# Retention in head pairs, V-products written turned, and the group norm moved into the gate

## The chip, the cores and the metric

One Trainium2 chip, of which the kernel uses one core. The metric is device time in microseconds (us) of one execution. In the profile PE is TensorE, PEld its weight load, DVE is VectorE, ACT is ScalarE, POOL is GpSimd and SP the queue that issues the weight transfers.

## The reference, cut to what matters

Two blocks of a transformer run over 256 positions of width 1024. The last quarter holds the layer around the change: a latent attention (MLA) of 8 heads and a two-directional retention of 8 heads, both fed by one input projection, joined before one output projection.

```python
proj = rms_norm(h, mix_norm) @ w_in           # c_q, c_kv, k_pe, r_q, r_k, r_v, r_g
# MLA, for each of 8 heads (q, k of 96, v of 64)
p = softmax((q_nope @ k_nope.T + q_pe @ k_pe.T) * MLA_SCALE)      # 256 x 256
a = p @ v
# retention, for each of 8 heads of 64: decayed scores, forward and backward in one mask
o = (q @ k.T * 64 ** -0.5 * decay) @ v_r
o = (o - mean(o)) * rsqrt(var(o) + EPS)       # over the 64 values of a head
r = silu(r_g) * o
h = h + concat([a, r]) @ w_o
h = h + 0.5 * swiglu_2(rms_norm(h, ffn2_norm), ...)               # FFN4, the last phase
```

All is float32. A product with a weight is made as three passes over a high and a low part.

## The kernel before, in words

Rows are in two tiles t = 0, 1 of 128. Each phase is a list of steps, `walk_latent` for the layer above; every engine walks the same list and issues, in that order, what it has to do in a step. So the list fixes the order of work on each engine, and a wait in a step holds everything behind it on that engine.

Weights come in chunks of 128 x 1024. SP fills 4 raw buffers, and issues the transfer for chunk c + 4 when chunk c has been split. A refill step ("R" for one chunk) makes on ACT `w_high` (L1035) and then on DVE `w_low` (L1301); the ring of split chunks has 12 places, and `freed` lists chunks that TensorE has used with row tile 1, whose places wait for a refill. Counted from the first chunk of the latent layer, its input projections use chunks 0 to 22, `w_o` chunks 23 to 30, FFN4's first gate-and-up block 31 to 34, the second 35 to 38, and the first down block 39 and 40.

Steps of the layer: X(i, t, c) is one chunk of an input projection (6 matmuls of 512 columns); MS(v), v = 0 to 7, the MLA scores of two heads of one row tile, into the PSUM tile `pG[v % 2]`; on DVE MS takes the row maxima (L1539, L1542); ME(v) the exponentials on ACT (L1238) into `mp`; MPT(v) turns `mp` on TensorE (L1641) and copies it (L1548, DVE); MPV(v) multiplies by V (L1913); MN(t) divides four products by the softmax sums at once; MAT(t) turns them and splits high from low. The loop over v issues:

```python
            for v in range(8):
                if v < 7: step("ME", v + 1)
                step("MPT", v)
                # one or two X chunks
                if v < 6: step("MS", v + 2)
                if v >= 1: step("MPV", v - 1)
```

with a refill at the start and after MS. After it follow RT (turn q and k of the retention), `decay` (3 exponentials on ACT and one product on POOL for each head), RS (scores of a head, L1939), RM (times the decay, DVE, L1569), RPV (times V, L1952), the group norm on DVE (GNmean, GNvar, GNout), RAT (turn the result, split), and between them Oc(t, kt), the output projection, one chunk each. RROPE is the rotation of q and k on POOL.

The program emits each float32 product as two TensorE instructions, so a count of x8 below stands for four products; a transposition, and each pass of a product with a weight, is one.

Of the kernel before, what the change touches and what calls it, by code (L numbers as in the profile page):

```python
# [27 lines left out]
F32 = mybir.dt.float32  # L28
# [7 lines left out]
P = 128  # L36
# [68 lines left out]
CONSTS = C_REL + 4 * P  # L105
# [302 lines left out]
def walk_latent(step, freed, open_end):  # L408
# [33 lines left out]
    step("MT", 0)  # L442
    projects(2, 1)
    step("U", 1)
    step("exp_table",)
# [11 lines left out]
    beside = [(3, 1, c) for c in range(1, 4)] + [(4, 0, c) for c in range(4)] + [(4, 1, c) for c in range(4)]  # L457
    project(*beside.pop(0))
    refill(step, freed, 1)
    for v in range(8):  # L460
        refill(step, freed, 1)
        if v < 7:
            step("ME", v + 1)
        step("MPT", v)
        for _ in range(min(1 + v % 2, len(beside))):
            project(*beside.pop(0))
        if v < 6:
            step("MS", v + 2)
        refill(step, freed, 1)
        if v == 6:  # L470
            step("gate", 0)
        if v == 7:
            step("RT", 0)
            step("MAT", 0)
# [6 lines left out]
    step("MN", 1)  # L481
    step("gate", 1)
    step("decay", 0)
    step("decay", 1)
    output(0, 0)
    step("MAT", 1)
    refill(step, freed)
    for hd in range(2, 8):
        step("decay", hd)
    step("silu",)  # L490
    step("RS", 0)
    step("RS", 1)
    for hd in range(8):
        step("RM", hd)
        if hd == 0:
            output(0, 1)
        step("RPV", hd)
        if hd < 6:
            step("RS", hd + 2)
        if hd == 4:  # L500
            step("GNmean", 0)
    step("GNvar", 0)
    step("GNmean", 1)
    step("GNvar", 1)
    step("GNout", 0)
    step("GNout", 1)
    for kt in range(2, 4):
        output(0, kt)
    for kt in range(3):
        output(1, kt)  # L510
    step("RAT", 0)
    output(1, 3)
    step("RAT", 1)
    refill(step, freed)
# [60 lines left out]
def build(nc, x_in, stream, consts_in, table_in, pos_in, posts_in, out):  # L575
    with ExitStack() as ctx:
# [75 lines left out]
        ttmp = [place(f"ttmp{i}", [P, 8, RHALF], F32, lat_at + i * 1024 if i < 3 else None) for i in range(4)]  # L652
# [3 lines left out]
        mo = [place(f"mo{t}", [P, 512], F32, mq_at + t * MLA_HEADS * QK * 4) for t in range(2)]  # L656
        mv = [place(f"mv{t}", [P, 512], F32) for t in range(2)]
        rqk_both = place("rqk", [P, 2, 1024], F32)
# [4 lines left out]
        sd = [place(f"sd{i}", [P, 2, SEQ], F32, p_at + i * 2 * SEQ * 4) for i in range(2)]  # L663
# [4 lines left out]
        dm_at = [lat_at, lat_at + 1536] + [mkT_at + 1536 * i for i in range(5)] + [mpT_at + 2048]  # L668
# [8 lines left out]
        rel = consts[:, C_REL:C_REL + 4 * P]  # L677
# [56 lines left out]
        x_out, lat_ss, lr_ready = (rows2(n) for n in ("x_out", "lat_ss", "lr_ready"))  # L734
        latT_psum, latf_ready, lath_ready, latT_ready = (rows2(n) for n in ("latT_psum", "latf_ready", "lath_ready", "latT_ready"))
        u_out, mqk_ready, mT_psum = (rows2(n) for n in ("u_out", "mqk_ready", "mT_psum"))
# [3 lines left out]
        mo_ready = rows2("mo_ready")  # L740
        rrope_done = rows2("rrope_done")
        rT_psum, rqT_ready, rkT_ready = rows2("rT_psum"), rows2("rqT_ready"), rows2("rkT_ready")
        dm_exp, dm_ready, rot_part = sem("dm_exp"), sem("dm_ready"), sem("rot_part")
        rs_psum, sd_ready, rpv_done = sem("rs_psum"), sem("sd_ready"), sem("rpv_done")
        rgate, silu_ready = rows2("rgate"), sem("silu_ready")
        gn_var, gn_r, ro_ready = sem("gn_var"), sem("gn_r"), sem("ro_ready")
# [101 lines left out]
        def _(pool):  # L848
# [114 lines left out]
            def LAT(t, ph):  # L963

                pool.wait_ge(lat_ss[t], 2)
                link(pool.tensor_scalar(lms[t][:, 0:1], lss[t][:, 0:1], 1.0 / Q_RANK, EPS, ALU.mult, ALU.add))
                link(pool.tensor_scalar(lms[t][:, 1:2], lss[t][:, 1:2], 1.0 / KV_RANK, EPS, ALU.mult, ALU.add))
                pool.tensor_tensor(lrr[t], lms[t], half_neg[:, 0:2], ALU.pow).then_inc(lr_ready[t], 1)

            def U(t, ph):  # L970
                if t == 1:

                    pool.wait_ge(latT_psum[1], 1)
                    pool.wait_ge(mqk_ready[1], 2)
# [22 lines left out]
            def GNvar(part, ph):  # L997

                g = gn[part]
                pool.wait_ge(gn_var, part + 1)  # L1000
                link(pool.tensor_scalar(g[:, 2, :], g[:, 1, :], 1.0 / HD, EPS, ALU.mult, ALU.add))
                pool.tensor_tensor(g[:, 3, :], g[:, 2, :], half_neg, ALU.pow).then_inc(gn_r, 1)
# [9 lines left out]
            steps = {f.__name__: f for f in (start, parts, finish, tail, rope, S, LAT, U, RROPE, decay, GNvar)}  # L1012
# [9 lines left out]
        def _(sc):  # L1022
# [178 lines left out]
            def LAT(t, ph):  # L1201
                sc.wait_ge(x_out[t], 1)
                sc.activation(junk[t][:, 0:Q_RANK], lat[t][:, 0:Q_RANK], ACT.Square, accum_out=lss[t][:, 0:1]).then_inc(lat_ss[t], 1)
                sc.activation(junk[t][:, Q_RANK:Q_RANK + KV_RANK], lat[t][:, Q_RANK:Q_RANK + KV_RANK], ACT.Square,
                              accum_out=lss[t][:, 1:2]).then_inc(lat_ss[t], 1)
                sc.wait_ge(latf_ready[t], 1)
                if t == 1:
                    sc.wait_ge(u_done0, 1)
                sc.activation(latTh[:], latf[:], ACT.Copy).then_inc(lath_ready[t], 1)

            def U(t, ph):
                if t == 1:
                    sc.wait_ge(w_freed, C_U + 3)
                    sc.wait_ge(mT_psum[0], 2)
                else:
                    sc.wait_ge(u_done0, 1)
                sc.wait_ge(lr_ready[t], 1)
# [7 lines left out]
            def MT(t, ph):  # L1225
                sc.wait_ge(mT_psum[t], 1)
# [4 lines left out]
            def ME(v, ph):  # L1231
                t, j = v // 4, v % 4
                sc.wait_ge(mmax_ready, v + 1)
# [6 lines left out]

            def RT(t, ph):
# [854 lines left out]
```

## Time and profile before

| | us |
|---|---|
| median of 3 runs | 1067.25 (1066.87 to 1067.92) |
| profiled execution, time | 1068.99 |
| profiled execution, span of the trace | 1067.1 |
| PE busy | 1056.3 (99%) |
| PEld busy | 873.2 (82%) |
| DVE busy | 656.3 (62%) |
| ACT busy | 559.4 (52%) |
| POOL busy | 104.8 (10%) |

The span runs from the first to the last instruction; the time of the execution also holds what lies around it, 1.9 us here. Busy time is the union of an engine's instructions. Matmuls are pipelined, so two in a row overlap and the distance of their starts is what one costs; the chain view shows these shares alone.

### The profile page before, as it was taken

How to read it: one execution, taken by the hardware profiler on the slowest of the kernel's cores; microseconds unless marked ns; L12 is line 12 of the kernel's file. 1: busy time of each engine (PE TensorE's matmuls, PEld its weight loads, DVE VectorE, ACT ScalarE, POOL GpSimd, SP SyncE). 2: the span in 40 equal slices, each digit the busy share in tenths (PEclk: the TensorE clock that was granted, in tenths of full speed). 3: DMA queues.
4: the chain of work that ended last, by engine and by line, in shares of the span. 5: the costliest groups of instructions: out<-in, count | busy, mean ns of one | idle time of the engine just before them, and what ended most of it. 6: DMA issues, size and time to landing. Idle time of an engine off the chain costs nothing.

```text
span 1067.1 us, 14824 instructions
## 1 busy us (share of the span) xinstructions
PE 1056.3 (99%) x5047; PEld 873.2 (82%) x5047; DVE 656.3 (62%) x932; ACT 559.4 (52%) x905; POOL 104.8 (10%) x194
## 2 busy tenths in 40 slices
PE   9999999999999999999999999999999999999997
PEld 6999888888877788888888888888888888888886
DVE  5867754546687775554667555466668674655544
ACT  5755644535677654454555445455576544444542
POOL 0035000000022040000000000000026110000001
PEclk9999999999999999999999999999999999999999
DMA  8563656555552354645555464555545133646441
GB/s 339 181 241 128 211 167 214 174 180 201 192 194 102 119 195 160 216 170 184 196 198 188 164 218 172 182 196 198 178 158 178 61 128 109 213 161 215 169 147 40
DMA packets 51884, 187.81 MB, mean 176 GB/s; under 512 B 5808, under 2 KB 5952, under 8 KB 51840
## 3 DMA queue, kind: packets, MB, share of 16 engines
q1 hardware_dynamic: 50688, 183.79, 49.5%
q0 software_dynamic: 864, 3.07, 1.0%
q8 instruction: 27, 0.44, 0.2%
q10 hardware_dynamic: 288, 0.37, 0.1%
q14 instruction: 17, 0.14, 0.0%
HBM read 186.15 MB, written 1.05 MB: 175 GB/s over the span
## 4 chain that ended last, share of the span: by engine, by line
PE 94%; DVE 3%; ACT 1%; issue 0%; DMA 0%; POOL 0%; POOLq 0%; DVEq 0%; SPq 0%; ACTq 0%
PE pG L1636 17%; PE pG L1638 17%; PE pG L1637 17%; PE pD L1636 11%; PE pD L1638 11%; PE pD L1637 11%; PE pT L1641 3%; DVE w_low L1301 1%; PE pG L1641 1%; PE pG L1658 1%; PE pT L1952 1%; PE pG L1939 1%; PE pD L1913 1%; PE pT L1779 1%; PE pD L1641 1%; PE pG L1894 1%
## 5 line engine op out<-in xcount | busy, mean ns | idle before, releaser
L1301 DVE TENSOR_TENSOR w_low<-raw,w_high 128x1024 fp32r<-128x1024 f32 x340 | 412.6, 1232 | 119.6 <-ACT w_high L1035 107.3
L1035 ACT ACTIVATE w_high<-raw 128x1024 fp32r<-128x1024 f32 x340 | 351.5, 1055 | 78.4 <-PE pG L1638 66.5
L1636 PE MATMUL pG<-w_high,xTh 128*128 128x512 f32 (+1 forms) x816 | 320.3, 393 | 0.1
L1638 PE MATMUL pG<-w_high,xTl 128*128 128x512 f32 (+1 forms) x816 | 312.7, 383 | 0.0
L1637 PE MATMUL pG<-w_low,xTh 128*128 128x512 f32 (+1 forms) x816 | 312.2, 383 | 0.0
L1638 PEld LDWEIGHTS pG<-w_high,xTl 128*128 128x128 f32 x816 | 153.2, 188 | 28.2
L1637 PEld LDWEIGHTS pG<-w_low,xTh 128*128 128x128 f32 x816 | 153.7, 188 | 25.6
L1636 PEld LDWEIGHTS pG<-w_high,xTh 128*128 128x128 f32 x816 | 153.3, 188 | 25.6 <-DVE xTl L1334 0.4
L1636 PE MATMUL pD<-w_high,aTh 128*128 128x512 f32 x384 | 150.9, 393 | 0.0
L1638 PE MATMUL pD<-w_high,aTl 128*128 128x512 f32 x384 | 150.0, 390 | 0.0
L1637 PE MATMUL pD<-w_low,aTh 128*128 128x512 f32 x384 | 149.5, 389 | 0.0
L1120 ACT ACTIVATE gate<-pG,stat 128x256 f32<-128x256 f32 x104 | 49.2, 474 | 169.2 <-PE pG L1638 167.0
L1140 ACT ACTIVATE aTh<-pT 128x256 fp32r<-128x256 f32 x88 | 33.7, 383 | 150.8 <-PE pT L1641 150.8
L1440 DVE TENSOR_TENSOR aTl<-pT,aTh 128x256 fp32r<-128x256 f32 x88 | 37.3, 424 | 119.0 <-ACT aTh L1140 119.0
L1421 DVE SCALAR_TENSOR_TENSOR act<-pG,stat,gate 128x256 f32<-128x256 f32 x88 | 42.3, 481 | 95.7 <-ACT gate L1120 95.6
L1638 PEld LDWEIGHTS pD<-w_high,aTl 128*128 128x128 f32 x384 | 72.1, 188 | 15.1
L1636 PEld LDWEIGHTS pD<-w_high,aTh 128*128 128x128 f32 x384 | 72.1, 188 | 14.1
L1637 PEld LDWEIGHTS pD<-w_low,aTh 128*128 128x128 f32 x384 | 72.2, 188 | 14.1
L1636 PE MATMUL pD<-w_high,xTh 128*128 128x512 f32 (+1 forms) x160 | 64.6, 404 | 0.0
L1638 PE MATMUL pD<-w_high,xTl 128*128 128x512 f32 (+1 forms) x160 | 62.0, 388 | 0.0
L1637 PE MATMUL pD<-w_low,xTh 128*128 128x512 f32 (+1 forms) x160 | 61.8, 386 | 0.0
L1641 PE MATMUL pT<-consts,act 128*128 128x128 f32 x192 | 37.8, 271 | 0.2 <-DVE act L1421 0.2
(266 smaller groups left out, 834.1 us busy)
## 6 DMA issues: line engine op xcount, KB each, us to landing
raw<-in_stream SPq DMA_DIRECT2D x340, 512.0 KB, 4.3
post<-in_posts POOLq DMA_DIRECT2D x5, 512.0 KB, 5.1
early<-in_stream SPq DMA_DIRECT2D x4, 512.0 KB, 12.0
first_w<-in_stream SPq DMA_DIRECT2D x3, 512.0 KB, 5.4
h<-in_x SPq DMA_DIRECT2D x2, 512.0 KB, 5.0
out<-hg SPq DMA_DIRECT2D x3, 256.0 KB, 2.3
consts<-in_consts POOLq DMA_DIRECT2D x1, 416.0 KB, 4.6
out<-hg ACTq DMA_DIRECT2D x1, 256.0 KB, 2.7
```

Source lines behind the costliest of these rows:

```text
L1035: sc.activation(w_high[:, slot(static):slot(static) + CHUNK], raw_of(static), ACT.Copy).then_inc(w_high_done, 1)
L1120: sc.activation(gate[t][:], pG[t][:, 0:256], ACT.Copy if ph.mixer else ACT.Silu, scale=rr[t]).then_inc(gate_ready[t], 1)
L1140: sc.activation(aTh[t][:].rearrange("p k r -> p (k r)"), pT[t][:, 0:256], ACT.Copy).then_inc(ah_ready[t], 1)
L1301: ve.tensor_tensor(w_low[:, slot(static):slot(static) + CHUNK], raw_of(static), w_high[:, slot(static):slot(static) + CHUNK].bitcast(F32), ...
L1421: ve.scalar_tensor_tensor(act[t][:], pG[t][:, 256:512], rr[t], gate[t][:], ALU.mult, ALU.mult).then_inc(act_ready[t], 1)
L1440: ve.tensor_tensor(aTl[t][:].rearrange("p k r -> p (k r)"), pT[t][:, 0:256], aTh[t][:].rearrange("p k r -> p (k r)").bitcast(F32), ALU.sub ...
L1636: pe.matmul(dst, ah, hi, start=start, stop=False)
L1637: pe.matmul(dst, ah, lo, start=False, stop=False)
L1638: return pe.matmul(dst, al, hi, start=False, stop=stop)
L1641: return pe.transpose(dst, src, ident)
L1658: mm = pe.matmul(pG[t][:, 0:MIX.cols], hg[t][:, kt * P:(kt + 1) * P], first_w[:, kt * MIX.cols:(kt + 1) * MIX.cols], start=kt == 0, stop=k ...
L1779: mm = pe.matmul(pT[p][:, P * keys * x:P * keys * (x + 1)], qT[t][part, 4 * a + first + x, :], kT[part, a, 0:P * keys], start=True, stop=True)
```

## The change

Four things are done together in the latent layer.

1. RS and RPV take two heads in one step. The scores alternate between the row halves of the array (heads 2i and 2i+1 lie on partitions 0 to 63 and 64 to 127), the products with V between the column halves, with V as the stationary operand and 256 moving columns, so that the result is written turned. MPV is written turned in the same way, with 128 moving columns; MAT needs no turning any more, and the transpositions of the MLA result go.
2. The softmax sums then lie on the wrong axis, so MN(v) divides `mp` before it is turned, for each v: a reciprocal of 128x2 and a product of 128x512 on DVE, and MPT(v) on TensorE waits for it. The copy of the turned `mp` moves from DVE to ACT.
3. V of the retention is centred over the head before it is used (VC: a reduction and a scaling on DVE, a subtraction on POOL). The variance is made from squares (ACT) by TensorE products with a column of 1/64 (VAR); the inverse root goes into the gate, the gate is turned (GT), and RY multiplies it by the turned product.
4. The list of steps is written anew: one X chunk in a turn of the loop instead of one or two, refills only after the odd turns, four X chunks between the retention steps, `decay` for four heads inside the loop, RROPE between the projections, and refills limited to given numbers later on.

```diff
     step("LAT", 0)
+    step("RROPE", 0, 0)
...
     step("U", 0)
+    step("RROPE", 0, 1)
...
     projects(3, 0)
+    step("VC", 0)
     step("MT", 1)
-    for t in range(2):
-        for part in range(2):
-            step("RROPE", t, part)
     project(3, 1, 0)
...
-    beside = [(3, 1, c) for c in range(1, 4)] + [(4, 0, c) for c in range(4)] + [(4, 1, c) for c in range(4)]
+    beside = [(3, 1, c) for c in range(1, 4)] + [(4, 0, c) for c in range(4)]
     project(*beside.pop(0))
     refill(step, freed, 1)
     for v in range(8):
-        refill(step, freed, 1)
         if v < 7:
             step("ME", v + 1)
+        step("MN", v)
         step("MPT", v)
-        for _ in range(min(1 + v % 2, len(beside))):
+        for _ in range(min(1, len(beside))):
             project(*beside.pop(0))
         if v < 6:
             step("MS", v + 2)
...
         if v >= 1:
             step("MPV", v - 1)
-        if v == 4:
-            step("MN", 0)
+        if v == 3:
+            step("VC", 1)
+        if 2 <= v < 6:
+            step("decay", v - 2)
+        if v == 6:
+            step("MAT", 0)
+        refill(step, freed, v % 2)
+    step("RT", 0)
+    step("gate", 0)
     step("MPV", 7)
+    project(4, 1, 0)
     step("RT", 1)
+    project(4, 1, 1)
+    step("decay", 4)
+    step("decay", 5)
+    step("RS", 0)
+    step("RM", 0)
+    project(4, 1, 2)
+    step("decay", 6)
+    step("RPV", 0)
+    step("RS", 1)
+    step("RM", 1)
+    step("decay", 7)
+    project(4, 1, 3)
+    step("RPV", 1)
+    step("RS", 2)
     step("gate", 1)
+    step("SQ", 0)
+    step("RM", 2)
+    step("MAT", 1)
     output(0, 0)
...
+    step("RPV", 2)
+    step("RS", 3)
+    step("RM", 3)
     step("silu",)
...
+    output(0, 1)
+    step("VAR", 0)
     step("GNvar", 0)
...
+    step("RPV", 3)
+    step("SQ", 1)
+    step("GNout", 0)
+    refill(step, freed, 1)
+    output(0, 2)
+    step("VAR", 1)
     step("GNvar", 1)
...
+    output(0, 3)
     step("GNout", 1)
...
+    refill(step, freed, 1)
     for kt in range(3):
         output(1, kt)
-    step("RAT", 0)
+    step("GT", 0)
+    step("RY", 0)
     output(1, 3)
-    step("RAT", 1)
-    refill(step, freed)
+    step("GT", 1)
+    step("RY", 1)
+    step("RL", 0)
+    step("RL", 1)
+    refill(step, freed, 2)
     for kt in range(4, 8):
         output(0, kt)
...
+            def MN(v, ph):
+                t, j = v // 4, v % 4
+                ve.wait_ge(mp_ready, 2 * (v + 1))
+                chain(ve.reciprocal(lrec[t][:, 2 * j:2 * j + 2], lsum[t][:, 2 * j:2 * j + 2]))
                 joined()
...
+                ve.tensor_tensor(mp[v % 2][:], mp[v % 2][:], lrec[t][:, 2 * j:2 * j + 2].unsqueeze(2).broadcast_to([P, 2, SEQ]),
+                                 ALU.mult).then_inc(mn_ready, 1)
...
             def MPT(v, ph):
-                pe.wait_ge(mp_ready, 2 * (v + 1))
+                pe.wait_ge(mn_ready, v + 1)
...
+                for kt in range(2):
+                    for x in range(2):
+                        hd = 2 * j + x
+                        mm = pe.matmul(pD[t][HD * x:HD * (x + 1), 512 + P * j:512 + P * (j + 1)], mv[kt][:, HD * hd:HD * (hd + 1)],
+                                       mpT[v % 2][:, (2 * x + kt) * P:(2 * x + kt + 1) * P], start=kt == 0, stop=kt == 1)
...
+            def RS(i, ph):
...
                 for jt in range(2):
...
+                    for x in range(2):
+                        part = slice(HD * x, HD * (x + 1))
+                        mm = pe.matmul(pG[x][:, SEQ * jt:SEQ * (jt + 1)], rkT[part, i, P * jt:P * (jt + 1)], rqT[part, i, :],
+                                       start=True, stop=True)
...
+            def VAR(part, ph):
...
+                for i in range(2):
+                    for t in range(2):
+                        first = 8 * part + 4 * t + 2 * i
+                        mm = pe.matmul(pD[1][:, first:first + 2], sq[part][:, SEQ * i + P * t:SEQ * i + P * (t + 1)], half_mean,
+                                       start=True, stop=True)
```

`refill(step, freed, n)` refills at most n chunks of `freed`, and without n all of them; the first such full refill of FFN4 stands in its first step, `walk_block_step(ph, 0)`, behind T(0, 0), the turning of the first activation of row tile 0.

## Rows read from the trace of the kernel before

**Rows 1.** The page: busy time of each engine, and the chain's shares by engine

```profile
PE 1056.3 (99%) x5047; PEld 873.2 (82%) x5047; DVE 656.3 (62%) x932; ACT 559.4 (52%) x905; POOL 104.8 (10%) x194
PE 94%; DVE 3%; ACT 1%; issue 0%; DMA 0%; POOL 0%; POOLq 0%; DVEq 0%; SPq 0%; ACTq 0%
```

**Rows 2.** Busy time by stretch; columns: us, PE, PEld, DVE, ACT, POOL (instructions), PEclk, DMA share, GB/s

```profile
798.00:834.00 36.00, 35.86 (x218) 31.34 (x218) 31.18 (x42) 22.13 (x50) 20.18 (x19) 1.00 0.49 175
...
1050.00:1067.00 17.00, 10.43 (x53) 8.67 (x51) 7.62 (x16) 4.76 (x12) 3.06 (x3) 0.94 0.17 63
```

**Rows 3.** The chain that ended last, three stretches; columns: start us, us, what

```profile
355.46 1.06 PE pT L1779 x8
356.52 1.01 PE pG L1804 x8
...
811.47 0.87 PE pG L1894 x4
812.33 0.84 PE pD L1913 x8
813.17 0.44 PE pT L1641 x4
...
841.43 1.06 PE pG L1939 x4
842.49 1.03 PE pT L1952 x8
```

**Rows 4.** Timeline of PE in the MLA loop; start us, us, engine, line, operation

```profile
801.71 0.66 PE L1641 MATMUL pT<-consts,mp 128*128 128x128 f32 x4
...
809.48 0.61 PE L1641 MATMUL pT<-consts,mp 128*128 128x128 f32 x4
...
811.31 1.03 PE L1894 MATMUL pG<-mkT,mqT 96*128 96x256 f32 x4
...
819.75 1.03 PE L1894 MATMUL pG<-mkT,mqT 96*128 96x256 f32 x4
```

**Rows 5.** Timeline of DVE in the same loop

```profile
802.64 2.89 DVE L1301 TENSOR_TENSOR w_low<-raw,w_high 128x1024 fp32r<-128x1024 f32 x2 [0.66 <-ACT w_high L1035]
...
820.82 0.69 DVE L1539 TENSOR_REDUCE mx<-pG 128x2 f32<-128x512 f32 x1 [1.25 <-PE pG L1894]
...
821.62 1.22 DVE L1301 TENSOR_TENSOR w_low<-raw,w_high 128x1024 fp32r<-128x1024 f32 x1
822.75 0.20 DVE L1552 RECIPROCAL lrec<-lsum 128x8 f32<-128x8 f32 x1
822.99 0.69 DVE L1555 TENSOR_TENSOR mo<-pD,lrec 128x512 f32<-128x512 f32 x1
```

**Rows 6.** Timelines, hand-overs: DVE to PE, then PE to ACT

```profile
834.44 0.69 DVE L1555 TENSOR_TENSOR mo<-pD,lrec 128x512 f32<-128x512 f32 x1
...
835.18 0.66 PE L1641 MATMUL pD<-consts,mo 128*128 128x128 f32 x4 [0.22 <-DVE mo L1555]
...
859.63 0.66 PE L1641 MATMUL pG<-consts,rqk 128*128 128x128 f32 x4
...
860.33 0.60 ACT L1278 ACTIVATE xTh<-pG 128x512 fp32r<-128x512 f32 x1 [15.27 <-PE pG L1641]
```

**Rows 7.** Timelines: start of Oc(0, 4), then the start of FFN4

```profile
861.87 0.48 PE L1636 MATMUL pD<-w_high,xTh 128*128 128x512 f32 x1
...
880.64 0.48 PE L1636 MATMUL pG<-w_high,xTh 128*128 128x512 f32 x1
...
888.92 0.38 PE L1641 MATMUL pT<-consts,act 128*128 128x128 f32 x2
...
883.04 1.05 ACT L1035 ACTIVATE w_high<-raw 128x1024 fp32r<-128x1024 f32 x1
...
884.12 1.22 DVE L1301 TENSOR_TENSOR w_low<-raw,w_high 128x1024 fp32r<-128x1024 f32 x1 [0.53 <-ACT w_high L1035]
```

**Rows 8.** The page: weight transfers, KB each, median us to landing

```profile
raw<-in_stream SPq DMA_DIRECT2D x340, 512.0 KB, 4.3
```

More of the change, by code:

```diff
@@ L442, in walk_latent @@
     step("MT", 0)
+    step("RROPE", 1, 0)
     projects(2, 1)
     step("U", 1)
+    step("RROPE", 1, 1)
     step("exp_table",)
@@ L651, in build @@
         lat = [place(f"lat{t}", [P, LATENT], F32) for t in range(2)]
-        ttmp = [place(f"ttmp{i}", [P, 8, RHALF], F32, lat_at + i * 1024 if i < 3 else None) for i in range(4)]
+        at[0] = lat_at + 4 * P * 8
         mq_at = at[0]
@@ L655, in build @@
         mk = place("mk", [P, MLA_HEADS, QK], F32)
-        mo = [place(f"mo{t}", [P, 512], F32, mq_at + t * MLA_HEADS * QK * 4) for t in range(2)]
+        mv_at = at[0]
         mv = [place(f"mv{t}", [P, 512], F32) for t in range(2)]
+        sq = [place(f"sq{i}", [P, 512], F32, mv_at + 2048 * i) for i in range(2)]
+        roS = place("roS", [P, 4, SEQ], F32, lat_at)
         rqk_both = place("rqk", [P, 2, 1024], F32)
@@ L666, in build @@
         mpT = [place(f"mpT{i}", [P, 4 * P], F32) for i in range(2)]
[L668 removed]
+        sd = [place(f"sd{i}", [P, 2, 2, SEQ], F32, p_at + i * 4096) for i in range(2)]
+        yo = [place(f"yo{t}", [P, 512], F32, p_at + 2048 * t) for t in range(2)]
+        ttmp = [place(f"ttmp{i}", [P, 8, RHALF], F32, (p_at + 2048, p_at + 3072, mpT_at + 2048, mpT_at + 3072)[i]) for i in range(4)]
+        dm_at = [mq_at + 1536 * i for i in range(4)] + [mkT_at + 1536 * i for i in range(4)]
         dm = [place(f"dm{i}", [P, 3 * P], F32, dm_at[i]) for i in range(8)]
@@ L1010, in finish @@
                 pool.tensor_tensor(rr[1], ms[1], half_neg[:, 0:1], ALU.pow).then_inc(end_r, 1)
-            steps = {f.__name__: f for f in (start, parts, finish, tail, rope, S, LAT, U, RROPE, decay, GNvar)}
+            steps = {f.__name__: f for f in (start, parts, finish, tail, rope, S, LAT, VC, RROPE, decay, GNvar)}
             in_loop = ("G", "D", "T", "Y", "R")
@@ L1938, in RS @@
+            def RS(i, ph):
+                if i == 0:
+                    pe.wait_ge(rqT_ready, 2)
+                    pe.wait_ge(rkT_ready, 2)
+                else:
+                    pe.wait_ge(sd_ready, 4 * i)
                 for jt in range(2):
-                    mm = pe.matmul(pG[hd % 2][:, SEQ * jt:SEQ * (jt + 1)], rkT[part, hd // 2, P * jt:P * (jt + 1)],
-                                   rqT[part, hd // 2, :], start=True, stop=True)
+                    for x in range(2):
+                        part = slice(HD * x, HD * (x + 1))
+                        mm = pe.matmul(pG[x][:, SEQ * jt:SEQ * (jt + 1)], rkT[part, i, P * jt:P * (jt + 1)], rqT[part, i, :],
+                                       start=True, stop=True)
@@ L1956, in MAT @@
-            def MAT(t, ph):
-                pe.wait_ge(mo_ready[t], 1)
-                for k in range(4):
-                    mm = turned(pD[t][:, 512 + P * k:512 + P * (k + 1)], mo[t][:, P * k:P * (k + 1)])
-                mm.then_inc(catT_psum[t], 1)
-            def RAT(t, ph):
-                pe.wait_ge(ro_ready, 2)
-                for k in range(4):
-                    mm = turned(pG[t][:, P * k:P * (k + 1)], rqk[t][:, P * k:P * (k + 1)])
+                    pe.wait_ge(vc_ready, 2)
@@ new lines, in RPV @@
+                for jt in range(2):
+                    for x in range(2):
+                        hd = 2 * i + x
+                        mm = pe.matmul(pT[i // 2][HD * x:HD * (x + 1), SEQ * (i % 2):SEQ * (i % 2 + 1)], rv[jt][:, HD * hd:HD * (hd + 1)],
+                                       sd[i % 2][:, x, jt, :], start=jt == 0, stop=jt == 1)
+                mm.then_inc(rpv_done, 1)
+            def VAR(part, ph):
+                pe.wait_ge(sq_ready, part + 1)
+                if part == 0:
+                    pe.wait_ge(rgate, 2)
+                else:
+                    pe.wait_ge(gn_var, 1)
+                for i in range(2):
[3 more added lines that the diff above has]
+                                       start=True, stop=True)
+                mm.then_inc(var_psum, 1)
@@ L1977, in _ @@
             steps = dict(start=start, turn=turn, first=first, G=G, D=Dn, T=T, proj=proj, QKT=QKT, S=S, PT=PT, PV=PV, O=O, X=X, LAT=LAT_,
-                         U=U, MT=MT, MS=MS, MPT=MPT, MPV=MPV, RT=RT, RS=RS, RPV=RPV, MAT=MAT, RAT=RAT, Oc=Oc)
+                         U=U, MT=MT, MS=MS, MPT=MPT, MPV=MPV, RT=RT, RS=RS, RPV=RPV, VAR=VAR, GT=GT, Oc=Oc)
             walk(pe, lambda name, *a, ph=None: steps[name](*a, ph) if name in steps else None)
@@ L2061, in shape_constants @@
     dist = j - i
-    c[:, C_REL:C_REL + 4 * P] = np.concatenate(
+    c[:, C_REL:C_HALF] = np.concatenate(
         [np.maximum(dist, 0), dist + P, np.maximum(-dist, 0), P - dist], axis=1)
+    for x in range(2):
+        c[HD * x:HD * (x + 1), C_HALF + x] = 1.0 / HD
     return c
```

258 lines of the change are left out of this document (105 added, 153 removed).

## The prediction

> **What bounds the kernel now.** I read the page first. TensorE is busy in 99% of the span and holds 94% of the chain that ended last; DVE is busy in 62%, ACT in 52% [rows 1]. Then the stretches around the change: in the MLA loop (798 to 834 us) PE is busy in 35.86 of 36 us at the full granted clock, while DVE is close behind with 31.18 and POOL works 20.18 [rows 2]. So the kernel runs as long as TensorE's instructions take, as long as nothing they wait for is late. The change must be read twice: what TensorE's work becomes, and whether what feeds it still comes in time. For the first I take the chain view, which gives what each group costs alone; for the second the timelines of PE and DVE, with each engine's steps in the order of the new list.
>
> **TensorE's work.** Scores of one head cost 1.06 us (x4), the product with V of one head 1.03 (x8) [rows 3]. The attention of the first block already alternates halves of the array: there twice as many instructions of the same width cost 1.06 (row halves) and 1.01 (column halves, 256 moving columns) [rows 3]. So RS goes from 8 x 1.06 to 4 x 1.06, a gain of 4.2 us, and RPV from 8 x 1.03 to 4 x 1.01, 4.2. MPV, now 0.84, has no like: 128 moving columns in column halves. Below it stands half of 0.84, 0.42, above it 0.84; I take 0.6: four instructions of 256 columns cost 0.87, so eight of 128 would too; half of it is 0.44, and the attention's pair lies 0.14 above its own half (1.01 against 0.87) [rows 3]. That gives 8 x 0.24 = 1.9. MAT's eight transpositions go, 2 x 0.44 = 0.9 [rows 3]. VAR adds 2 x 8 instructions whose stationary operand is 128 x 128 and which hardly move a column; the nearest row is MPV's 0.84 for 8, so +1.7 (at the least 0.4, if nearly all of that were columns). GT replaces RAT one for one. Sum: 4.2 + 4.2 + 1.9 + 0.9 - 1.7 = 9.5 us less for TensorE.
>
> Between whole array and halves a changeover shows: four score instructions of the retention (half the rows) cost 1.06 beside MLA's 0.87, and RPV 1.03 beside MPV's 0.84, 0.19 each [rows 3]. The Trainium skill, TensorEngine Tiling (Array Packing), Key Properties, says that changing the tiling mode drains TensorE. That speaks against a change that puts a column-half product into each turn of a loop of whole-array work; my 0.6 has 0.14 of it, and by that rule, with a drain at both edges, it would be 8 x 0.19 = 1.5 us more, six of the eight in the shadow of the wait below.
>
> **The new wait in the MLA loop.** Before, MPT(v) needed only the exponentials. Now it needs MN(v), and DVE works in the order of the list: MN(v), MS(v+2), on odd turns a refill, MN(v+1). The row maxima of MS(v+2) cannot begin before TensorE has made these scores, and MN(v+1), whose exponentials are long ready, is queued behind them; behind MPT(v+1) on TensorE is queued everything else. One turn, from MPT(v) to MPT(v+1):
> - MPT(v), one X chunk, start of MS(v+2): 811.31 - 809.48 = 1.83 [rows 4];
> - start of MS to the maxima on DVE: 820.82 - 819.75 = 1.07; maxima and scaling to the next DVE instruction: 0.80 [rows 4, 5];
> - reciprocal to product 0.24; product 0.69, the same size as mo's; hand-over to PE 0.05 [rows 5, 6].
>
> Sum 4.68 us. TensorE's work in it is 1.83 + 0.87 + 0.6 = 3.3, so it stands about 1.4 us in each turn. A refill between adds 1.13 (821.62 to 822.75) in the turns that follow v = 1, 3, 5; VC(1) at v = 3 adds 0.80, by the like pair of instructions. MPT(0) to MPT(6): 6 x 4.68 + 3 x 1.13 + 0.80 = 32.3 us. ACT (exponentials, copy, decay, w_high) has about 3.5 of work a turn, so it is not what ends.
>
> The start is late too: refill 24 stands before MN(0) on DVE. It began at 802.64 and holds 1.13, so MPT(0) starts at 802.64 + 1.13 + 0.24 + 0.69 + 0.05 = 804.75, where it started at 801.71 [rows 4, 5]. MN(6) is done at 804.7 + 32.3 = 837.0.
>
> **From MN(6) to Oc(0, 4).** At v = 6 DVE has MAT(0)'s low part ahead of MN(7), and that waits for ACT, whose copies wait for MPT(6): hand-over 0.05, PE to ACT 0.70 (859.63 to 860.33), two ACT copies 0.50 and 0.60, 0.05, low part 0.60, MN(7) 0.24 + 0.69 + 0.05 = 3.5 us until MPT(7) [rows 5, 6]. From there the work of TensorE rules, since four X chunks and the Oc chunks lie between the retention steps: transpositions of MPT(7), RT and GT 7 x 0.44 = 3.1; MPV 2 x 0.6 = 1.2; 12 chunks of 1.40 (1.83 less 0.44 for the turning) = 16.8; RS 4.2; RPV 4.0; VAR 1.7; 31.0 in all. Waits beside it: RT(1), whose banks are copied behind refill 28, 0.3; the handing over between RS, RM and RPV, 0.6; and RL(0), the low part that Oc(0, 4) needs, which is queued on DVE behind RY(1) and so behind GT(1): 0.70 + 0.60 + 0.69 + 0.05 less the turning, 1.6. Together 3.5 + 31.0 + 2.5 = 37.0, so Oc(0, 4) starts at 874.0 instead of 861.87 [rows 7]. That is +12.1 us, with the 9.5 us of saved work already in it: the waits take some 21.
>
> **The refills put off.** Counting `freed` along both lists: before, the layer splits up to chunk 41 ahead of FFN4's first block; after, at the same place, only up to 35, and the full refill behind T(0, 0) then does seven, 36 to 42, where it did one. The second gate-and-up block needs 36 at once. In before's time (880.64 the start of that block, 888.92 T(0, 1)) [rows 7]: chunk 35 lasts until 882.1; w_high of 36 begins at 883.04 and w_low ends at 884.12 + 1.22 = 885.3, a stall of 3.2. Chunks 37 to 39 lie in the raw buffers and come each 1.13. The transfer for 40 goes out when 36 is split, lands 4.3 later [rows 8], and after 1.06 and 1.22 is ready at 891.9; PE has come to it at 890.8. Chunk 42 follows at 894.2, and only behind it in DVE's queue stands the activation that T(0, 1) turns: 894.2 + 0.48 + 0.05 = 894.7 for 888.92. That is +5.8; if the transfers were there already it would be 3.8, with a landing 1 us slower 6.9. FFN4 is bound by TensorE and gives nothing back.
>
> **Moved at no cost.** RROPE on POOL now lies beside the projections; LAT(1) is queued behind two of its four parts on POOL, which fit between the projections, and it takes POOL off the loop, where two w_low took 2.89 instead of 2.3 [rows 5] (all of it lies in the 20.18 us of POOL [rows 2]). If LAT(1) were late it would cost one part, some 5 us. VC on POOL and four `decay` on ACT lie in the shadow of the waits. SP issues the same transfers in the same order, the constants grow by two columns.
>
> **Sum.** +12.1 + 5.8 = +17.9. Against the profiled execution that is 1068.99 + 17.9 = 1086.9 (its span 1067.1 + 17.9 = 1085.0); it ran 1.7 above the median, so against the median 1067.25 + 17.9 = 1085.2. I say 1085. Its own range is 1080 to 1090, from the bounds above (MPV and VAR 1, the transfers 2 down and 1 up, contention of VC(1) with DVE 0.6, waits in the retention 2).
>
> **Rivals.**
> - *Arithmetic alone.* TensorE has its maxima and MN early enough, and only its work counts: 1067.25 - 9.5 = 1057.8, faster. It decides if a turn from MPT to MPT stays at 3.3 to 3.4 us, so if DVE's part after MS took 0.6 instead of 2.85. The busy shares speak for it (DVE 62%), the order of DVE's queue against it. Chance 7%.
> - *The loop is late, the refills are hidden.* The seven refills find cover in FFN4 (DVE is busy a good half of the time): 1067.25 + 12.1 = 1079.4. It would need T(0, 1) not to stand behind chunk 42. 12%.
> - *The clock falls.* All through the loop the granted clock is 1.00, which is 2.4 GHz; at the end of the kernel, once TensorE has finished, it is 0.94 in the mean [rows 2]. If it went to 1.2 GHz for the six turns, PE's share of a turn, 1.83 + 0.87, would double: 6 x 2.7 = 16.2 on top, 1101. The stalls are of 1.4 to 3.5 us with work between them. The Trainium skill, TensorE: Matmul & The Clock Gate, the section on HAM oscillation, has repeated waits throttle the array; no stretch of before with such waits shows it. 6%.
> - *More late than I see*: a wait on ACT, LAT(1), or in the retention, some 5 to 8 us on top: 1092. 10%.
> - The forecast, 65%.
>
> **Numbers.** The measurement tells a difference from none at about 0.2% (2.1 us). Faster 8%: the arithmetic case and a little for gains I have not counted. Same 2%: it would need both delays to be a third of what I count. Slower 90%. The range reaches from 1077 (the refills hidden, with a margin) to 1093 (one more wait), and leaves out the clock and the arithmetic case.
>
> **What would show it.** In the trace after: starts of `pT<-consts,mp` 4.7 us apart, 5.8 after odd turns, each with PE idle until DVE `mp`; MPV about 0.6; RS and RPV x8 at about 1.05; 12 us more to the start of Oc(0, 4); seven w_low in a row behind the first activation of FFN4, with PE idle for 3 us in `pG`. Wrong it would be if the MPT starts lay 3.4 apart, or if the DVE product on `mp` came before the maxima of the next scores.

## The result, and the profile after

The changed kernel took 1097.22 us (median of 4, 1095.22 to 1098.18) beside 1067.59 for the kernel before (median of 4, 1066.87 to 1068.48): a ratio of 1.0275, with an interval of 1.0257 to 1.0293. The forecast was 1085, with a range to 1093; the direction was right, the size was not: +29.6 us instead of +17.9. The profiled execution took 1097.25 us, with a span of 1095.3.

The page, busy time and the chain's shares by engine, to be read against [rows 1]:

```profile
PE 1059.1 (97%) x5023; PEld 867.6 (79%) x5023; DVE 658.3 (60%) x932; ACT 567.8 (52%) x917; POOL 105.1 (10%) x194
PE 89%; DVE 7%; ACT 2%; issue 1%; DMA 1%; POOL 0%; POOLq 0%; ACTq 0%; DVEq 0%; SPq 0%
```

TensorE has 24 instructions less, yet it is busy for longer. DVE had 3% of the chain and now has 7%. What TensorE waited for between 740 and 930 us (columns: engine and line, releaser: us in total, times, longest):

```profile
PE pT L1663 <- DVE mp L1588: 17.5, 8, 3.8
PE pG L1658 <- DVE w_low L1340: 3.1, 1, 3.1
PE pT L1663 <- DVE act L1460: 2.3, 2, 2.1
PE pG L1663 <- DVE mq L1552: 1.7, 1, 1.7
PE pD L1658 <- DVE xTl L1644: 1.4, 1, 1.4
```

That is 26.0 us of waits with DVE as the releaser. All eight MPT wait for MN's product on `mp`. PE's timeline of three turns (against [rows 4]):

```profile
805.50 0.66 PE L1663 MATMUL pT<-consts,mp 128*128 128x128 f32 x4 [2.81 <-DVE mp L1588]
...
810.19 0.66 PE L1663 MATMUL pT<-consts,mp 128*128 128x128 f32 x4 [1.78 <-DVE mp L1588]
810.60 0.48 PE L1658 MATMUL pD<-w_high,xTh 128*128 128x512 f32 x1
810.91 0.59 PE L1659 MATMUL pD<-w_low,xTh 128*128 128x512 f32 x1
811.30 0.63 PE L1660 MATMUL pD<-w_high,xTl 128*128 128x512 f32 x1
811.72 0.63 PE L1658 MATMUL pD<-w_high,xTh 128*128 128x512 f32 x1
...
813.00 1.70 PE L1916 MATMUL pG<-mkT,mqT 96*128 96x256 f32 x4
...
817.62 1.01 PE L1663 MATMUL pT<-consts,mp 128*128 128x128 f32 x4 [2.33 <-DVE mp L1588]
```

The first turn, from MPT(0) to MPT(1), lasts 4.69 us. In the second the matmuls of the X chunk come to start 0.42 apart, where at the full clock it is 0.23, and MS(3) lasts 1.70, where it lasts 1.03 in the kernel before [rows 4]. Busy time by stretch (columns as in [rows 2]; the last but two is the granted clock):

```profile
811.00:813.00 2.00, 2.00 (x6) 1.54 (x5) 0.00 (x0) 0.48 (x1) 0.00 (x0) 0.50 0.00 0
...
822.00:831.00 9.00, 4.20 (x31) 3.03 (x30) 5.68 (x11) 4.56 (x13) 2.39 (x2) 1.00 0.03 5
831.00:834.00 3.00, 2.84 (x10) 2.36 (x11) 0.10 (x1) 1.57 (x4) 0.68 (x2) 0.57 0.44 160
...
846.00:850.00 4.00, 3.38 (x18) 2.72 (x19) 1.22 (x2) 1.68 (x3) 0.00 (x0) 0.50 0.00 0
```

0.50 is the lower level, 1.2 GHz. TensorE falls to it behind some of the waits, and the work of that turn takes nearly twice as long; in other turns it keeps 1.00, which is 2.4 GHz. The DVE timeline shows the order in the queue that makes the wait (against [rows 5]): maxima first, then reciprocal and product.

```profile
808.45 0.69 DVE L1578 TENSOR_REDUCE mx<-pG 128x2 f32<-128x512 f32 x1 [3.00 <-PE pG L1916]
...
809.25 0.16 DVE L1586 RECIPROCAL lrec<-lsum 128x2 f32<-128x2 f32 x1
809.44 0.69 DVE L1588 TENSOR_TENSOR mp<-mp,lrec 128x512 f32<-128x512 f32 x1
```

**A common zero.** Executions differ by up to 2 us before the layer begins. So all starts below count from the layer's first instruction on TensorE, the turning of h: 741.57 us before, 740.71 after. In the timeline after, these are the starts that the table uses:

```profile
740.71 0.60 PE L1663 MATMUL pG<-consts,h 128*128 128x128 f32 x4
...
846.62 1.11 PE L1663 MATMUL pT<-consts,mp 128*128 128x128 f32 x4 [2.11 <-DVE mp L1588]
...
882.81 0.50 PE L1658 MATMUL pD<-w_high,xTh 128*128 128x512 f32 x1 [1.38 <-DVE xTl L1644]
...
917.13 0.44 PE L1663 MATMUL pT<-consts,act 128*128 128x128 f32 x2 [2.08 <-DVE act L1460]
```

Starts in us after that zero, from one profiled execution each; MPT(0) to MPT(7) is the loop, T(0, 1) the place in FFN4 behind which nothing differs any more:

| kernel | MPT(0) | MPT(7) | Oc(0, 4) | T(0, 1) | time, median |
|---|---|---|---|---|---|
| before | 60.1 | 87.5 | 120.3 | 147.4 | 1067.6 |
| after | 64.8 | 105.9 | 142.1 | 176.4 | 1097.2 |
| sums first | 64.8 | 87.9 | 121.7 | 156.0 | 1076.9 |
| gaps filled | 64.8 | 101.3 | 135.1 | 169.2 | 1089.5 |
| refills earlier | 64.8 | 109.3 | 145.8 | 172.9 | 1089.1 |
| rotation small | 62.9 | 105.6 | 141.8 | 175.5 | 1095.4 |
| chunk behind scores | 64.8 | 100.5 | 135.8 | 169.6 | 1091.4 |
| two mended | 64.8 | 87.9 | 121.7 | 148.8 | 1070.7 |
| four mended | 60.8 | 83.9 | 118.2 | 145.3 | 1065.9 |
| halves in turn | 60.8 | 83.9 | 118.3 | 145.4 | 1064.9 |
| same half | 60.8 | 83.9 | 120.1 | 147.2 | 1069.0 |
| refill ahead of decay | 60.8 | 83.1 | 115.8 | 142.9 | 1063.8 |

The difference at T(0, 1), 29.1 us, is the whole of what was measured (29.6). Against the forecast: up to MPT(0) 4.65 instead of 3.0, from there to Oc(0, 4) 17.15 instead of 9.1, from there to T(0, 1) 7.27 instead of 5.8. So 11.2 us are to be explained on top of the 17.9, and the 17.9 themselves are to be tested.

### The profile page after: what moved, and what is told of

It reads as the page before. It is cut to its first block, busy times and chain, and to the rows that moved or that the text cites. A ratio compares the mean times of both kernels' runs of the same rounds, so it can differ in the third digit from the quotient of the medians.

```text
span 1095.3 us, 14788 instructions
## 1 busy us (share of the span) xinstructions
PE 1059.1 (97%) x5023; PEld 867.6 (79%) x5023; DVE 658.3 (60%) x932; ACT 567.8 (52%) x917; POOL 105.1 (10%) x194
## 4 chain that ended last, share of the span: by engine, by line
PE 89%; DVE 7%; ACT 2%; issue 1%; DMA 1%; POOL 0%; POOLq 0%; ACTq 0%; DVEq 0%; SPq 0%
PE pG L1658 16%; PE pG L1660 16%; PE pG L1659 16%; PE pD L1658 11%; PE pD L1660 10%; PE pD L1659 10%; DVE w_low L1340 3%; PE pT L1663 3%; PE pG L1680 1%; PE pG L1663 1%; ACT w_high L1058 1%; PE pG L1916 1%; PE pT L1801 1%; DVE mp L1588 1%; DMA raw<-in_stream 1%
```

## The experiments

Ten kernels were run. Beside them the kernel before had medians of 1067.5 to 1068.0, and the ratios are to those. "After" is the changed kernel.

**1. Sums first.** MN(v + 1) stands ahead of MS(v + 2), so that on DVE the product no longer waits behind the maxima.

```diff
+    step("MN", 0)
     for v in range(8):
...
-        step("MN", v)
         step("MPT", v)
...
             project(*beside.pop(0))
+        if v < 7:
+            step("MN", v + 1)
         if v < 6:
             step("MS", v + 2)
```

> The changed kernel with one step moved: the division MN(v+1) stands in the list ahead of the row maxima of MS(v+2), so on VectorE it no longer waits for scores that TensorE has not made. Theory A (the queue order on VectorE is what makes TensorE stand in the loop): turns of 3.3 to 3.7 us instead of 4.7 to 7.4, MPT(0) to MPT(7) about 25 us instead of 41.1, the granted clock back to 1.00 in the loop, and the time 15 to 18 us below that of the changed kernel, 1079 to 1082. Theory B (VectorE or ScalarE has too much work in a turn, whatever the order): turns stay above 4.5 us and the time within 3 us of 1097. If only the clock were at fault and the stalls harmless, it would gain at most the 6 us that the slow stretches of the loop cost.

Measured: 1076.85 us (1076.09 to 1077.11), ratio 1.0081 (1.0064 to 1.0098), 20.4 less than after. PE's timeline:

```profile
805.52 0.66 PE L1665 MATMUL pT<-consts,mp 128*128 128x128 f32 x4 [2.80 <-DVE mp L1590]
...
808.26 0.60 PE L1665 MATMUL pT<-consts,mp 128*128 128x128 f32 x4
...
811.63 0.66 PE L1665 MATMUL pT<-consts,mp 128*128 128x128 f32 x4
```

Turns of 2.7 to 3.8 us instead of 4.7 to 7.4; between 804 and 846 us PE is busy for 38.48 us at a clock of 1.00, where it was 26.41 at 0.87. The place of one step in the list cost two thirds of the loss. It is more than the waits that vanished: PE waited 17.5 us for `mp` and now waits 4.8, 12.7 less. The other 7.7 us, which also put the time below the 1079 to 1082 that I expected, are a second effect that the waits bring about, and the next run looks for it.

**2. Gaps filled.** The list is that of after; 37 useless products of 128x256, whose results nobody reads, run on TensorE in its waits.

```diff
         if v >= 1:
             step("MPV", v - 1)
+        step("gap", v)
...
+                for _ in range({-1: 6, 0: 3, 1: 5, 2: 3, 3: 8, 4: 3, 5: 5, 6: 4}.get(v, 0)):
+                    pe.matmul(dst, ident, rel[:, 0:256], start=True, stop=True)
```

> The changed kernel with useless products (128x128 by 256 columns, 0.43 us each, results never read) put on TensorE into the places of the loop where it stands: 3, 5, 8 or 6 of them according to the wait, 37 in all. No wait is taken away. Theory A (the clock fell because TensorE stood, and cost time on top of the stalls): the granted clock stays at 1.00 up to the first retention step, the turns return to the 4.7, 5.8 and 6.6 us worked out at the full clock, and the time falls by 6 to 9 us, to 1088 to 1091, although TensorE has 16 us more work. Theory B (the longer turns come from contention or a slower ScalarE, and the clock only shows it): the time stays at 1097 or rises by up to 3 us.

Measured: 1089.53 us (1089.29 to 1089.72), ratio 1.0202 (1.0185 to 1.0219). With work added, it is 7.7 us faster than after. The stretches of the loop, first of after, then of this kernel:

```profile
804.00:846.00 42.00, 26.41 (x136) 19.68 (x136) 16.83 (x35) 18.52 (x50) 4.18 (x5) 0.87 0.15 51
```
```profile
804.00:846.00 42.00, 40.99 (x240) 31.27 (x239) 18.44 (x35) 20.85 (x52) 4.18 (x5) 1.00 0.16 52
```

The clock stays at 1.00, and the turns last 4.69, 5.84, 4.83, 7.19, 4.83 and 5.76 us, 33.1 in all for a forecast of 32.3 (4.68, 5.81, 4.68, 6.61, 4.68, 5.81). So the wait was sized rightly. Of the 0.8 us between, 0.65 is one instruction: in the turn with VC(1) the product on `mp` takes 1.34 us instead of 0.69, beside VC's and decay's work on POOL, here as in after:

```profile
829.76 1.34 DVE L1588 TENSOR_TENSOR mp<-mp,lrec 128x512 f32<-128x512 f32 x1
```

The clock cost 37.8 - 33.1 = 4.6 us in the loop and, from MPT(7) to Oc(0, 4), 36.2 - 33.8 = 2.4: 7.0 together; the medians have 7.7. The Trainium skill, TensorE: Matmul & The Clock Gate, the section on HAM oscillation, tells of a loop whose waits, for a DMA and of some 3 to 5 us, throttle the array anew each time. The trace agrees that such waits do it, but here they are for VectorE, most are shorter (1.2 to 3.8 us), and the clock does not fall behind each of them. In FFN4 it falls too, behind the wait for `w_low` (0.59 in 906 to 909 us of after), but there the chain of after runs over the transfer and the refills, and TensorE waits again at T(0, 1), so the lower clock costs nothing that shows.

**3. Refills earlier.** A refill behind each of four retention steps, and all that are left behind RL(1), so that FFN4 finds its chunks split.

```diff
     step("decay", 7)
+    refill(step, freed, 1)
     project(4, 1, 3)
     step("RPV", 1)
+    refill(step, freed, 1)
...
     step("RL", 1)
-    refill(step, freed, 2)
+    refill(step, freed)
```

> The changed kernel with four refills put between the retention steps and a full refill after RL, so that chunks up to 41 are split before FFN4's first block, as in the kernel before. Theory A (the seven refills behind the first activation of FFN4 cost TensorE two stalls and a stretch of slow clock): from Oc(0, 4) to T(0, 1) of FFN4 27 us instead of 34.3, and the time 6 to 7.5 us lower, 1090 to 1091. Theory B (the delay is made up elsewhere, or the refills now hold up the retention on VectorE): within 2 us of 1097, or up to 3 us above.

Measured: 1089.05 us (1086.5 to 1093.26), ratio 1.0189 (1.0172 to 1.0206), 8.2 less than after. The wait for `w_low` is gone, and that for `act` is 0.2 instead of 2.3; `mp` keeps its 17.3. From Oc(0, 4) to T(0, 1) it takes 27.1 us, as before (27.05), where after took 34.3: the burst of refills cost 7.2 us, and FFN4 covers none of it. The profiled execution was the slowest of the four, and its clock was 0.76 between 804 and 846 us, with the list of the loop unchanged; its first turn, from MPT(0) to MPT(1), took 7.17 us where after took 4.69. The four executions of this one kernel go from 1086.5 us at a mean clock of 0.994 to 1093.26 at 0.986. The clock doesn't fall at the same waits in each execution.

**4. Rotation small.** RROPE on POOL rotates one head of eight and leaves the others as they are; its steps stay in their places.

```diff
+                z, co, si = z[:, 0:1, :], co[:, 0:1, :], si[:, 0:1, :]
```

> The changed kernel with the rotation on GpSimd cut to one head of eight (the other heads of the retention stay unrotated): its 24 instructions shrink from 128x256 to 128x32 elements and no longer lie beside VectorE's work of U(1) and MT(1). Theory A (GpSimd's early rotation slows VectorE there and makes TensorE stand 1.7 us ahead of MT(1)): that stall goes and the time falls by 1.5 to 2.5 us, to about 1095. Theory B (the stall has another cause, the reordered projections): no change beyond 0.5 us.

Measured: 1095.42 us (1094.3 to 1097.41), ratio 1.0253 (1.0236 to 1.0271), 1.8 less than after. The four times overlap with those of after (1095.22 to 1098.18), so the medians alone don't show the gain; the trace does. MPT(0) starts at 62.9 instead of 64.8, 1.9 earlier, and that is the 1.7 us of PE's wait for `mq`; at T(0, 1) 1.0 of it is left in this execution. What made it is in the DVE timeline of after; the groups have 4 and 1 instructions:

```profile
783.77 6.78 DVE L1340 TENSOR_TENSOR w_low<-raw,w_high 128x1024 fp32r<-128x1024 f32 x4 [0.16 <-ACT w_high L1058]
790.47 0.70 DVE L1546 TENSOR_TENSOR mpT<-lat,trig 128x16 f32<-128x16 f32 x1
...
793.59 0.82 DVE L1547 TENSOR_TENSOR mpT<-mq,trig 128x128 f32<-128x128 f32 x1
```

and in that of the kernel with the small rotation:

```profile
784.89 2.36 DVE L1341 TENSOR_TENSOR w_low<-raw,w_high 128x1024 fp32r<-128x1024 f32 x2 [0.16 <-ACT w_high L1059]
...
792.66 0.28 DVE L1548 TENSOR_TENSOR mpT<-mq,trig 128x128 f32<-128x128 f32 x1
```

Beside POOL a `w_low` takes 1.7 us instead of 1.2, and of the six operations of 128x128 behind them two take 0.82 and 0.81, while the other four take 0.28 or 0.29 as in the small rotation. The Trainium skill, GPSIMD Engine Reference, Specifications, has GpSimd's memory interface shared with VectorE, in contention with instructions of two inputs; these have two, and the trace agrees.

**5. Chunk behind scores.** A weaker cure for the wait than the first: the X chunk of a turn goes behind MS(v + 2), so that the maxima can begin 1.4 us earlier.

```diff
         step("MPT", v)
-        for _ in range(min(1, len(beside))):
-            project(*beside.pop(0))
         if v < 6:
             step("MS", v + 2)
+        for _ in range(min(1, len(beside))):
+            project(*beside.pop(0))
```

> The changed kernel with another mend of the loop: the X chunk stands behind MS(v+2) instead of ahead of it, so that TensorE has 1.4 us of work while VectorE makes maxima and division; the order on VectorE stays as changed. Theory A (a turn is the chain MPT, MS, maxima, refill, division, and the chunk lay in it): turns of 3.3 to 3.5 us without a refill, 4.4 with one and about 5.3 with VC(1), MPT(0) to MPT(7) 27 to 29 us instead of 41.1, and the time 12 to 14 us below 1097, but 4 to 7 above the run with the division first. Theory B (the order of the maxima and the division alone matters): turns hardly shorter than 4.7 us.

Measured: 1091.44 us (1089.7 to 1092.9), ratio 1.0227 (1.0212 to 1.0243), only 5.8 less than after. I expected 12 to 14, with 27 to 29 us from MPT(0) to MPT(7); it took 35.7. Only the first turn shrinks as it should, to 3.7. The other two without a refill take 5.0 and 5.1 for an expected 3.3 to 3.5, though TensorE doesn't wait for `mp` in them: the clock is at its lower level for much of each.

```profile
816.00:820.00 4.00, 4.00 (x13) 2.86 (x11) 1.62 (x4) 2.59 (x8) 0.45 (x1) 0.57 0.39 135
828.00:832.00 4.00, 4.00 (x20) 2.92 (x19) 1.62 (x4) 2.38 (x8) 0.46 (x1) 0.73 0.01 3
```

The turns with a refill take 7.3, 6.0 and 5.3, for 4.4, 5.3 (with VC(1)) and 4.4. ACT and DVE of the second turn:

```profile
811.91 0.69 ACT L1222 ACTIVATE rv<-pD,stat 128x512 f32<-128x512 f32 x1 [1.83 <-PE pD L1660]
812.50 1.04 ACT L1058 ACTIVATE w_high<-raw 128x1024 fp32r<-128x1024 f32 x1
```
```profile
813.58 1.23 DVE L1340 TENSOR_TENSOR w_low<-raw,w_high 128x1024 fp32r<-128x1024 f32 x1 [2.15 <-ACT w_high L1058]
...
814.91 0.69 DVE L1588 TENSOR_TENSOR mp<-mp,lrec 128x512 f32<-128x512 f32 x1
```

The chunk that was put later ends an input projection, whose result ACT copies (`rv`); behind that copy ACT has `w_high`, behind `w_high` DVE has `w_low`, and behind it stands the product. In the sixth turn no such copy stands there, and the chain runs over ACT all the same: copy of the turned `mp`, three exponentials of `decay`, `w_high`, then `w_low` and the product. My expectation moved the chunk on TensorE and forgot what stands ahead of `w_high` on ACT: the same error as in the change itself, one engine further. And it had no term for the clock.

**6. Two and four mended.** The first is experiments 1 and 3 together. The second adds: refill 24 behind MS(2) instead of ahead of MN(0), RL(0) ahead of GT(1), and the last part of RROPE behind the rotation of `mq` and `mk`. So the second, called "four mended", differs from after in five places.

```diff
     project(*beside.pop(0))
-    refill(step, freed, 1)
     step("MN", 0)
...
             step("MS", v + 2)
+        if v == 0:
+            refill(step, freed, 1)
...
+    step("RL", 0)
     step("GT", 1)
     step("RY", 1)
-    step("RL", 0)
     step("RL", 1)
...
+                if t == 1 and part == 1:
+                    pool.wait_ge(mqk_ready[1], 2)
```

> The changed kernel with the division ahead of the row maxima (20.4 us by itself) and the refills between the retention steps (8.2 us by itself) together. Theory A (two separate delays, which add): the second still takes its two stalls and its slow stretch away, 6 to 8 us, so 1069 to 1071, within 0.4% of the kernel before. Theory B (the delays share a cause, such as the clock, so that the second is worth less once the first is gone): 1073 to 1077.

> As the run with both mended, and three small moves: refill 24 behind the first division instead of ahead of it, RL(0) ahead of GT(1) and RY(1), and the last quarter of GpSimd's rotation held until VectorE has done its own rotation for the MLA keys and queries. The stalls of TensorE that are left there are 2.8, 1.4 and 1.7 us. Theory A (each is a wait on the chain, and TensorE's saved 9.5 us then come through): 4 to 5 us below the run with both mended, 1064 to 1066, so just below the kernel before. Theory B (the held rotation runs into the exponentials or slows VectorE's refills at the start of the loop): no more than 2 us below it, so about the time of the kernel before.

Measured: 1070.68 us (1068.75 to 1071.6), ratio 1.0028 (1.0016 to 1.004), and 1065.87 (1063.94 to 1066.86), ratio 0.9982 (0.9973 to 0.9991). The second beats the kernel before, by 1.6 us. MPT(0) comes 4.0 us earlier than with two mended, and PE's wait for `mq` is gone. What is left of its waits, but for 0.2 us in FFN4, and its loop:

```profile
PE pT L1672 <- DVE mp L1597: 2.7, 3, 1.7
PE pD L1667 <- DVE xTl L1653: 0.3, 1, 0.3
```
```profile
800.00:830.00 30.00, 27.27 (x173) 20.60 (x172) 20.17 (x37) 21.94 (x58) 4.14 (x5) 0.94 0.23 85
```

**7. Halves in turn.** The kernel with four mended places, but RS, RPV and MPV issue all instructions of the one head and then all of the other, instead of alternating.

```diff
-                for jt in range(2):
-                    for x in range(2):
+                for x in range(2):
+                    for jt in range(2):
```

> As the run with four moves, but the two heads of RS, RPV and MPV follow one another instead of alternating between the halves of the array: the same products, the same waits, the same layout. Theory A (the halves work at the same time only because they alternate, and with TensorE the bound their gain is a gain in time): RS x8 about 2.1 us instead of 1.06, RPV x8 1.7 to 1.9 instead of 1.01, MPV x8 about 0.9 instead of 0.58, and the time 8 to 11 us above the run with four moves. Theory B (TensorE waits there for other engines anyway): less than 3 us above.

Measured: 1064.93 us (1063.34 to 1066.45), ratio 0.9975 (0.9966 to 0.9984), no slower than alternating. The theory that the gain needs the alternation fell. The chain view has the same costs:

```profile
832.47 1.07 PE pG L1971 x8
...
835.13 1.03 PE pT L1984 x8
```

**8. Same half.** So is there any overlap of halves at all? Both score products of RS read the upper row half; the scores of the odd heads are left out, and those of the even ones are made twice.

```diff
                         part = slice(HD * x, HD * (x + 1))
+                        part = slice(0, HD)
```

> The kernel with the four mended places, but both score products of a retention step (RS) read the upper row half of the array, partitions 0 to 63; the scores of heads 2i are made twice and those of heads 2i+1 left out. Eight instructions as before. Theory A, that the gain of a step comes from the two row halves working at the same time, in whatever order their instructions stand (so putting the heads one after the other did not lose it): each RS x8 costs 8 x 0.22 + 0.19 = 1.93 us in the chain instead of 1.06, four of them 3.5 us, so 1069.4 instead of 1065.9. Theory B, that an instruction on half of the array takes half the time by itself, or that a step of 8 costs no more than one of 4 for some other reason: RS x8 stays 1.06 and the time 1065.9 within 1.

Measured: 1069.03 us (1067.12 to 1070.39), ratio 1.001 (1.0001 to 1.0019), 3.2 more than with four mended, for an expected 3.5. The chain:

```profile
830.51 1.92 PE pG L1972 x8
832.43 0.43 PE pD L1667
```

1.92 us instead of 1.06: eight instructions on one half follow one another, and on two halves they run side by side, in either order of issue. The counting of RS in the prediction rests on this, and holds. For the column halves of RPV and MPV no run puts both heads on one half; for them it is only shown that the order doesn't matter (RPV 1.03 and 1.01). (In the trace the gap to the kernel with four mended is only 1.9 us: that one lost about 1.5 us to a lower clock behind its loop, which this execution didn't.)

**9. Refill ahead of decay.** The kernel with four mended places, with VC(1) at v = 4, a turn without a refill, and the refill of a turn ahead of `decay`.

```diff
-        if v == 3:
+        if v == 4:
             step("VC", 1)
-        if 2 <= v < 6:
-            step("decay", v - 2)
         if v == 6:
             step("MAT", 0)
         refill(step, freed, v % 2)
+        if 2 <= v < 6:
+            step("decay", v - 2)
```

> The kernel with the four mended places, and in the MLA loop the reduction and scaling of VC(1) a turn later (v = 4, which has no refill), and the refill of a turn ahead of the exponentials of decay. In the trace of the kernel with four mended places PE waited 2.7 us in three places for the product on mp, the product itself took 1.34 instead of 0.69 beside POOL, and the mean granted clock was 0.94 in 800 to 830. If those two orders are what ends last there, the waits fall to under 1 us and the clock stays at 1.00: 2 us less of waits and 1.3 to 1.8 us of clock, 1062 to 1063. If something else holds the loop (the copy of the turned scores on ACT), the time stays within 1 us of 1065.9.

Measured: 1063.78 us (1062.9 to 1064.02), ratio 0.9959 (0.9945 to 0.9972): 4.2 us faster than the kernel before, and the best of all. The waits for `mp` fell to 1.9 us only, less than expected, but the clock stays at 1.00:

```profile
PE pT L1672 <- DVE mp L1597: 1.9, 2, 1.2
```
```profile
800.00:830.00 30.00, 28.06 (x186) 21.22 (x184) 20.80 (x38) 23.61 (x64) 5.07 (x6) 1.00 0.29 100
```

## Why the prediction was right in direction and wrong in size

**TensorE's work: right unit by unit, but a changeover was left out.** The chain of the changed kernel has RS at 1.06 and RPV at 1.01 as forecast, VAR at 0.79 for 0.84 and MPV, at the full clock, at 0.59 for 0.6. What the sum didn't count is the instruction behind a half-array group. Three pieces of the chain of the last kernel:

```profile
804.00 0.44 PE pT L1672 x4
...
813.53 0.59 PE pD L1944 x8
814.12 0.59 PE pT L1672 x4
```

The transposition behind MPV costs 0.59 and not 0.44, and the first matmul of a chunk behind RS costs 0.43 and not 0.23. The prediction weighed the rule of the Trainium skill, TensorEngine Tiling (Array Packing), Key Properties, that a change of the tiling mode drains TensorE, and put 1.5 us on a drain at both edges. The rows agree that both edges cost something: the 0.59 of MPV holds the cost of coming in (0.15 above the half of 0.87), and the row behind it that of going out, 0.15 more, 8 x 0.15 = 1.2 us; for RS, with a chunk behind it four times, 0.8. (The kernel before paid 0.19 of this kind inside its RPV of 1.03, and the sum took that as saved.) So the arithmetic case was worth 7.5 us at most, not 9.5; behind RPV(3) and behind the second VAR the chunk costs 0.3 more. The best kernel gains 4.2; in its stretches from 800 to 900 us PE is idle 2.5 us to 0.5 before, and 1 us or so I have not placed.

**The wait in the loop: right.** A turn of 4.68 us was forecast, 4.69 was the first one measured; with the clock kept up the six turns took 33.1 instead of 32.3. The rest is the slow product beside POOL, 0.65, which the forecast had in its range (0.6 for VC(1)) and not in its sum, and 0.3 from the useless products themselves, which held two turns up by 0.15. Taking the wait away gave back 20.4 us.

**The step that failed: the clock was no term of the sum.** The prediction held it for a rival, with 6%, and priced it as all or nothing: 16.2 us on top, if every turn fell. What ran was between the two: some turns at half clock, some whole, and the same behind MPT(7), where two waits of 2 us and more are followed by 5 us at 0.50 to 0.52. That cost 7.0 us in the trace, shown by filling the gaps. It is the largest part of the 11.2, and with the gaps filled the time was 1089.5, inside the range. The sentence "no stretch of before with such waits shows it" was true, but it was no evidence for a clock that stays: in the kernel before TensorE never waits longer than 1.2 us at once.

**"Moved at no cost": wrong by 1.7 us.** I took RROPE between the projections for hidden, because LAT(1) finds its time on POOL. It did. But I had the row on which POOL makes two `w_low` last 2.89 instead of 2.3 [rows 5], and counted it only as a relief for the loop. The slowness went with POOL to the place where MT(1) waits for DVE. Up to MPT(0) the change cost 4.65 instead of 3.0, and the small rotation gave 1.9 back.

**The refills put off: right in kind, 1.5 us small.** Seven refills in a row, PE idle 3.1 us (forecast 3.2), T(0, 1) behind the last. The chain of after shows what the rest was:

```profile
905.07 3.50 DVE w_low L1340 x3
...
908.74 5.61 DMA raw<-in_stream
...
914.37 1.07 ACT w_high L1058
...
915.46 1.22 DVE w_low L1340
916.68 0.41 DVE act L1460
```

The last transfer took 5.61 us to land; I had put 4.3 [rows 8], the median over the kernel, though here four buffers come free, and four transfers go out, within some 4 us. That these slow each other is my reading; no run tests it. It is 1.3 of the 1.5; my bound for it, 1 us slower, was too narrow.

**From MN(6) to Oc(0, 4): right in the sum, partly by luck.** MPT(6) to MPT(7) took 3.36 for 3.5, and MPT(7) to Oc(0, 4) 33.8 for 33.5 with the gaps filled. But of these 33.8 TensorE is busy for 32.5, 1.5 more than the 31.0 counted (the changeovers), and idle for 1.4, 1.1 less than the 2.5 of waits forecast.

Together: 4.6 + 2.4 for the clock, 1.7 for POOL beside DVE, 1.3 for the landing, 0.8 for the rest of the loop, 10.8 of 11.2. The arithmetic rival was not what ran, but part of it is what the change could be: with its steps in better places the kernel takes 1063.8 us, where that rival had 1057.8.

## What to carry to other kernels

When a change puts a new step into an engine's queue, look at what stands ahead of it there and what that waits for: here one step, put on the wrong side of another, cost 20.4 of the 29.6 us. If the forecast has TensorE waiting repeatedly, put a term for the clock into the sum, between none and half clock for the work between the waits, and widen the range by it. And when work moves on GpSimd, price the VectorE instructions that it will now lie beside, with the slowed duration that the trace already shows elsewhere.

## What the runs showed of the hardware that I had not expected

- Waits of 1.2 to 3.8 us, with 3 us of work between, bring the granted clock to 0.50 for some microseconds and leave it at 1.00 at other times, with the same list of work: MPT(0) to MPT(1) took 4.69 us in after and 7.17 in refills earlier, whose loop is the same. The mean over 804 to 846 us was 0.87 and 0.76.
- 37 useless products in those waits made the kernel 7.7 us faster.
- Two row halves of the array overlap even when the four instructions of the one are issued ahead of the four of the other: 1.07 us, as when they alternate (1.06); eight on one half take 1.92.
- An elementwise VectorE instruction of 128x16 with two inputs took 0.70 us beside GpSimd, and 0.17 without it; others of the same size beside it took 0.16. One of 128x512 took 1.34 instead of 0.69.
